# The last unit of a long convolution in pieces of 256, 128 and 128 channels in place of two halves

## The chip, the cores and the metric

The kernel runs on one core of one Trainium2 chip. The metric is the device time of one execution in microseconds (us), lower is better; the median of several executions is compared. The engines are called as in the profile: PE multiplies matrices (TensorE; PEld is its loading of stationary operands), DVE is VectorE, ACT is ScalarE, POOL is GpSimd, and SP (SyncE) only issues transfers here.

## The reference, cut to what matters

Two transformer-like blocks over 1024 positions of width 1024. The first has a mixer and a mixture of experts; the second has a linear recurrence, two gated long convolutions, a merge of the two branches, and again a mixture of experts. The change lies in the long convolutions of the second block:

```python
def fftconv(u, k, bias):
    L = u.shape[1]
    U = jnp.fft.rfft(u, n=2 * L, axis=1)
    K = jnp.fft.rfft(k, axis=0)
    y = jnp.fft.irfft(U * K[None], n=2 * L, axis=1)[:, :L]
    return y + u * bias.astype(jnp.float32)
...
        z = v.astype(f32)
        for n, gate in enumerate((x1, x2)):
            k = bidir_kernel(filt[:, n, 0], filt[:, n, 1])
            z = gate.astype(f32) * fftconv(z, k, filt_bias[l, n])
        y_b = z.astype(dt) @ w_b_out[l]
```

`y_b` is then gated and added to the other branch, multiplied by `w_o`, added to `x`, normed, routed, and sent through 16 experts.

## The kernel before, in words

The whole program is one launch, stage after stage. Each stage gives every engine its own list of instructions; the engines meet only through semaphores, and each engine goes through its list in order. DVE operations that need the one before them are chained: `c.then` has the operation raise a semaphore, and the next waits for it.

A long convolution is done by a Fourier transform written as matrix products. The channels go in halves of HC = 512, and with two orders of convolution this makes NP = 4 passes (n = 0 to 3; pass n is order n // 2, half n % 2). The length is split in RADIX = 4 residues and the frequencies in HF = 2 halves `fh`. One "unit" is one pair (n, fh): PE makes the spectrum of the input, ACT copies it to SBUF, and DVE runs `unit_butterflies` (and for a filter made in place also `filter_butterflies`): it combines the residues, multiplies by the filter's spectrum K, and combines again. The result H lies in the place of the input spectrum U. For the last unit, n = 3 and fh = 1, that place is the tile `hytab_filt`. A unit's last DVE operation, line 4304, raises `h_ready`.

Then PE transforms back in `results(n)`, in BANKS = 8 banks per pass: bank = 2 * i + half. For the second order of convolution (n = 2, 3) bank 2i and 2i + 1 take the channels `bass.ts(i, P)`, the i-th 128 of the 512, for half of the residues. There are two PSUM buffers `inv_ps` for all banks, so a bank waits until the one two before it has been read out: `pe.wait_ge(*evicted(...))`. In pass 2 ACT reads them out, in pass 3 DVE does: `result(n, bank)`, line 4566, multiplies by the gate.

The last unit was already cut in two before the change: `butterflies` takes `at` and `width` (a range of channels). The unit's first half, channels 0 to 255, releases banks 0 to 3; its second half releases banks 4 to 7. Within the second half `unit_butterflies` calls `between(4)` to `between(7)` after each of its four big products (lines 4284 and 4286), and there DVE does `result(3, 0)` to `result(3, 3)`.

After the last unit DVE's list goes on with the start of the merge (`merge.begin`, lines 3535, 3543 and 3539, five operations of 1024 columns that have nothing to do with pass 3), and then with the results of banks 4 to 7, each followed by what `merge.after` gives:

```python
    def begin(m, dve):
        m.gate_z(dve, 0)
        m.gate_z(dve, 1)
        m.rest_of_first_w(dve)
        m.rest_of_z(dve, 0)
        m.gate_z(dve, 2)
```

When the eighth bank is done, PE begins the merge's product (line 2751). SP waits for all banks and for all results of DVE (`sp.wait_ge(z_ready, N_READY)`) before it issues the merge's transfers. POOL and ACT have nothing between PE and DVE in pass 3.

Of the kernel before, what the change touches and what calls it, by code (L numbers as in the profile page):

```python
# [3673 lines left out]
RADIX = 4  # L3674
HQ = T // RADIX
HJ = HQ // P
HF = HQ // P
HC = BANK
# [650 lines left out]
def hyena_phase(nc, block, m, tab, inputs, merge, v_x1, x2_T, z1):  # L4329


    NP = len(PASSES)
# [8 lines left out]
    def k_made(n, fh):  # L4341
        return place["K", n, fh] + RADIX
# [4 lines left out]
    BANKS = 2 * RADIX  # L4347
# [19 lines left out]
    fwd_copied, product_ready, h_ready = tab.fwd_copied, tab.product_ready, tab.h_ready  # L4367
# [9 lines left out]
    @block.sync  # L4377
    def _(sp):
        def load_u(n, fh):
            o, h = PASSES[n]  # L4380
            for i in SLOTS:
                v = RADIX * (HF * n + fh) + i
                before = v - N_CHUNKS

                sp.wait_ge(fwd_made, place["U", before // RADIX // HF, before // RADIX % HF] + before % RADIX + 1)
                if o and fh == 0:

                    made = RADIX * (n - 2) + i
                    sp.wait_ge(z_stored[made % 2], 16 * (made // 2 + 1))
                sp.dma_start(u[v % N_CHUNKS][:, :, :], residues(z1 if o else v_x1, RESIDUE[i], h)).then_inc(u_loaded[v % N_CHUNKS], 16)  # L4390

        for what, n, fh in program:
            if what == "U" and (n, fh) != (0, 0):
                load_u(n, fh)
                if n == 0:

                    sp.wait_ge(inputs.proj_made, inputs.n_proj)
                    tab.load_k(sp, K, 0, fh)
                elif n not in MADE:

                    sp.wait_ge(product_ready, HF * (n - 1) + fh + 1)
                    tab.load_k(sp, K, n, fh)
                if (n, fh) == (1, 0):
                    tab.load_inverse(sp)
                if (n, fh) == (2, 0):

                    for b in range(2):
                        sp.wait_ge(tab.filt_stored[b], 16 * (NT // 2))
                    sp.wait_ge(fwd_made, k_made(MADE[0], HF - 1))
                    sp.dma_start(filt[:, :, :, :, :], tab.filters).then_inc(filt_loaded, 16)  # L4410
# [37 lines left out]
    @block.tensor  # L4448
    def _(pe):
        def spectrum(q, fh, terms, src):  # L4450

            if q >= 2:

                pe.wait_ge(fwd_copied, q - 1)
            for c in (RE, IM):
                sums = [(kind, src(part, r, j), j) for kind, part, r in terms[c] for j in range(HJ)]
                for s, (kind, rhs, j) in enumerate(sums):
                    last = nc.tensor.matmul(fwd_ps[q % 2][:, c, :], tr[:, j, kind, fh, :], rhs, start=(s == 0), stop=(s == len(sums) - 1))
            last.then_inc(fwd_made, 1)

        def filter_spectra(n, fh):

            if n == MADE[0]:
                pe.wait_ge(tab.filt_ready, len(FILTER_STEPS))
            else:
                pe.wait_ge(filt_loaded, 16)
            for i in SLOTS:
                spectrum(place["K", n, fh] + i, fh, K_TERMS[i], lambda part, r, j: filt[:, part, j, r, :])

        def input_spectra(n, fh):  # L4470
            for i in SLOTS:
                v = RADIX * (HF * n + fh) + i
                r = RESIDUE[i]
                chunk = u[v % N_CHUNKS]
                pe.wait_ge(u_loaded[v % N_CHUNKS], 16 * (v // N_CHUNKS + 1))
                spectrum(place["U", n, fh] + i, fh, ([(COS_OF[r], 0, r)], [(SIN_OF[r], 0, r)]), lambda part, r, j: chunk[:, j, :])

        def results(n):
            o, h = PASSES[n]
            H = [U_of(n, fh) for fh in range(HF)]  # L4480

            pe.wait_ge(h_ready, HF * (n + 1))
            for bank in range(BANKS):
                i, half = bank // 2, bank % 2
                e = BANKS * n + bank
                if n == NP - 1 and bank == BANKS // 2:

                    pe.wait_ge(h_ready, HF * NP + 1)
                if e >= 2:

                    pe.wait_ge(*evicted((e - 2) // BANKS, (e - 2) % BANKS))
                out = inv_ps[e % 2]
                terms = [(fh, c) for fh in range(HF) for c in (RE, IM)]
                if o == 0:
                    for fh, c in terms:
                        last = nc.tensor.matmul(out[:, :], inv[:, fh, RESIDUE[i], c, bass.ts(half, P)], H[fh][:, i, c, :],
                                                start=((fh, c) == terms[0]), stop=((fh, c) == terms[-1]))
                else:
                    for k in range(2):
                        r = 2 * half + k  # L4500
                        for fh, c in terms:
                            last = nc.tensor.matmul(out[:, bass.ts(k, HQ)], H[fh][:, RESIDUE[r], c, bass.ts(i, P)], inv[:, fh, r, c, :],
                                                    start=((fh, c) == terms[0]), stop=((fh, c) == terms[-1]))
                last.then_inc(inv_made, 1)

        pe.wait_ge(tab.tr_loaded, 16 * HJ)
        pe.wait_ge(inputs.rows_ready, inputs.n_rows)
        pe.wait_ge(tab.filt_ready, len(FILTER_STEPS))
        for what, n, fh in program:
            if what == "K":  # L4510
                filter_spectra(n, fh)
            elif what == "U":
                if (n, fh) != (0, 0):
                    input_spectra(n, fh)
            else:
                if n == 0:
                    pe.wait_ge(tab.inv_loaded, 16)
                    pe.wait_ge(inputs.raw_ready, inputs.n_raw)
                results(n)
# [29 lines left out]
    @block.vector  # L4549
    def _(dve):  # L4550
        c = inputs.unit

        def result(n, bank):

            o = PASSES[n][0]
            i, half = bank // 2, bank % 2
            e, chunk = BANKS * n + bank, RADIX * n + i
            if o == 0:
                dve.wait_ge(gate_loaded[chunk % 2], 16 * (chunk // 2 + 1))
                part, made = z[chunk % 2][:, bass.ts(half, HC)], inv_ps[e % 2][:, :]  # L4560
            else:
                dve.wait_ge(x2_loaded[i], 16)
                part = merge.z.whole[:, RADIX + i, :].rearrange("p (q r) -> p r q", r=RADIX)[:, bass.ts(half, 2), :]
                made = inv_ps[e % 2][:, :].rearrange("p (r q) -> p r q", r=2)
            dve.wait_ge(inv_made, e + 1)
            dve.tensor_tensor(part, made, part, ALU.mult).then_inc(z_ready, 1)

        def butterflies(n, fh, back, first_bank=0, at=0, width=HC):

            g = HF * n + fh
            k, x = (w[:, :, :, bass.ds(at, width)] for w in (K[fh][:, :, :, :], U_of(n, fh)))
            by = cross[:, :, :, bass.ds(at, width)]

            def back_to(bank):
                if back is not None and bank >= first_bank:
                    result(back, bank - first_bank)

            def filter_made(dve):  # L4580
                dve.wait_ge(fwd_copied, k_made(n, fh))
                filter_butterflies(c, k)

            def filter_loaded(dve):
                dve.wait_ge(tab.k_loaded[fh], 16 * (n // HF + 1))

            k_ready = filter_made if n in MADE else filter_loaded
            if n in MADE and place["K", n, fh] < place["U", n, fh]:
                k_ready(dve)
                k_ready = lambda dve: None  # L4590
            dve.wait_ge(fwd_copied, u_made(n, fh))
            unit_butterflies(c, tab, g, k, x, by, width, k_ready, back_to, at != 0)

        dve.wait_ge(inputs.conv_ready, inputs.n_conv)
        for n in range(1, NP):
            butterflies(n - 1, 1, 0 if n - 1 == 1 else None)
            butterflies(n, 0, n - 1 if n - 1 == 1 else None)
        butterflies(NP - 1, 1, None, width=HC // 2)
        butterflies(NP - 1, 1, NP - 1, first_bank=4, at=HC // 2, width=HC // 2)
        merge.begin(dve)  # L4600
        for bank in range(BANKS // 2, BANKS):
            result(NP - 1, bank)
            merge.after(dve, bank)
# [302 lines left out]
```

## Time and profile before

| what | value |
|---|---|
| median of 3 runs | 3942.96 us (3939.01 to 3943.96) |
| the profiled execution | 3944.96 us, its span 3943.2 us |
| mean granted clock of PE | 0.973 |
| PE busy | 3710.8 us, 94% of the span |
| DVE busy | 2842.8 us, 72% |
| ACT busy | 1857.6 us, 47% |

The span is the time from the first to the last instruction that the profiler recorded; the profiled execution's own time is 1.76 us above it. The table is over the whole program, and the stage of the change is some 75 us of it, from about 2500 to 2575 us. There the trace is read in order of time: a row of the timeline has its start, its length, engine, line, operation, output <- inputs, shapes and count; a bracket at its end tells how long its engine was idle before it and what ended that. Like instructions that follow each other are merged in one row, xN being their number. In the profile one fp32 matmul is two records.

### The profile page before, as it was taken

What the parts mean: (1) busy time and instruction counts of PE and PEld (TensorE: products, weight loads), DVE (VectorE), ACT (ScalarE), POOL (GpSimd) and SP (SyncE); (2) the same over time, 40 slices, a digit from 0 to 9 for tenths busy, and PEclk for the clock granted to TensorE, in tenths of its full rate; (3) what the DMA queues carried; (4) which work ended last, traced back from release to release, by engine and by line L of the source; (5) the groups of instructions that cost most, each with busy time, mean ns of one, the idle gap of its engine ahead of it and who ended that gap; (6) DMA issues with size and microseconds to landing.
All of it is one profiled execution on the core that took longest, in us unless ns stands there. A gap on an engine that the chain in (4) does not pass through costs nothing. (4 is left out here: it accounts for less than half of the span.)

```text
span 3943.2 us, 42184 instructions
## 1 busy us (share of the span) xinstructions
PE 3710.8 (94%) x16780; PEld 2853.3 (72%) x16780; DVE 2842.8 (72%) x2581; ACT 1857.6 (47%) x1719; POOL 264.3 (7%) x281
## 2 busy tenths in 40 slices
PE   8989998799999799999999989899499999999998
PEld 3557776688888677777887634587288888888886
DVE  2655445889888675655345899954799898889887
ACT  3243431687777334443011111210377777777776
POOL 0000000100000200000000000000000101010100
PEclk9999999899999899999999999899799999999999
DMA  3003024899998632223344515143599999999998
GB/s 119 6 14 114 22 77 170 322 419 415 417 414 348 235 124 69 67 67 102 97 122 142 200 58 192 54 160 129 215 371 385 384 389 382 387 381 389 385 385 311
DMA packets 367168, 891.04 MB, mean 226 GB/s; under 512 B 21994, under 2 KB 118609, under 8 KB 357556
## 3 DMA queue, kind: packets, MB, share of 16 engines
q1 hardware_dynamic: 323796, 758.12, 51.7%
q0 software_dynamic: 26896, 97.17, 7.0%
q10 hardware_dynamic: 16336, 33.82, 2.2%
q8 instruction: 97, 1.59, 0.2%
q14 instruction: 43, 0.35, 0.0%
HBM read 788.65 MB, written 100.40 MB: 225 GB/s over the span
## 5 line engine op out<-in xcount | busy, mean ns | idle before, releaser
L2342 DVE TENSOR_TENSOR moe_w_rest<-moe_w_w,moe_upper 128x2048 fp32r<-128x2048 f32 x384 | 862.4, 2288 | 132.3 <-ACT moe_upper L2251 66.4
L2243 ACT ACTIVATE moe_upper<-moe_w_w 128x2048 fp32r<-128x2048 f32 x192 | 357.4, 1909 | 229.2 <-PE moe_y_ps L2207 103.2
L2342 DVE TENSOR_TENSOR moe_w_rest<-moe_w_w,moe_upper_w 128x2048 fp32r<-128x2048 f32 x192 | 430.6, 2284 | 14.0 <-ACT moe_upper_w L2261 13.9
L2261 ACT ACTIVATE moe_upper_w<-moe_w_w 128x2048 fp32r<-128x2048 f32 x192 | 357.5, 1910 | 116.5 <-PE moe_up_ps L2181 74.7
L2251 ACT ACTIVATE moe_upper<-moe_w_w 128x2048 fp32r<-128x2048 f32 x192 | 356.7, 1911 | 3.0 <-DMA moe_w_w<-in_w_up_dram 2.8
L2181 PE MATMUL moe_up_ps<-moe_upper,moe_x_upper 128*128 128x512 f32 x768 | 308.4, 402 | 0.0
L2181 PE MATMUL moe_gate_ps<-moe_upper,moe_x_upper 128*128 128x512 f32 x768 | 300.5, 391 | 4.7 <-DVE moe_x_rest L2355 4.7
L2181 PE MATMUL moe_gate_ps<-moe_upper,moe_x_rest 128*128 128x512 f32 x768 | 300.1, 391 | 0.0
L2181 PE MATMUL moe_up_ps<-moe_upper,moe_x_rest 128*128 128x512 f32 x768 | 299.9, 391 | 0.0
L2181 PE MATMUL moe_gate_ps<-moe_w_rest,moe_x_upper 128*128 128x512 f32 x768 | 299.9, 390 | 0.0
L2181 PE MATMUL moe_up_ps<-moe_w_rest,moe_x_upper 128*128 128x512 f32 x768 | 298.9, 389 | 0.0
L2207 PE MATMUL moe_y_ps<-moe_upper_w,moe_hidT_upper 128*128 128x512 f32 x760 | 295.9, 389 | 1.9 <-DVE moe_hidT_rest L2360 1.9
L2207 PE MATMUL moe_y_ps<-moe_upper_w,moe_hidT_rest 128*128 128x512 f32 x760 | 295.7, 389 | 0.0
L2207 PE MATMUL moe_y_ps<-moe_w_rest,moe_hidT_upper 128*128 128x512 f32 x760 | 295.7, 389 | 0.0
L2181 PEld LDWEIGHTS moe_gate_ps<-moe_upper,moe_x_upper 128*128 128x128 f32 x768 | 144.9, 189 | 35.6 <-DVE moe_x_rest L2355 5.5
L2181 PEld LDWEIGHTS moe_up_ps<-moe_upper,moe_x_rest 128*128 128x128 f32 x768 | 144.1, 188 | 31.7
L2181 PEld LDWEIGHTS moe_gate_ps<-moe_w_rest,moe_x_upper 128*128 128x128 f32 x768 | 145.0, 189 | 30.1
L2181 PEld LDWEIGHTS moe_gate_ps<-moe_upper,moe_x_rest 128*128 128x128 f32 x768 | 144.8, 189 | 30.3
L2207 PEld LDWEIGHTS moe_y_ps<-moe_upper_w,moe_hidT_upper 128*128 128x128 f32 x760 | 142.7, 188 | 32.1 <-DVE moe_hidT_rest L2360 2.7
L2181 PEld LDWEIGHTS moe_up_ps<-moe_w_rest,moe_x_upper 128*128 128x128 f32 x768 | 144.6, 188 | 27.3
L2207 PEld LDWEIGHTS moe_y_ps<-moe_upper_w,moe_hidT_rest 128*128 128x128 f32 x760 | 142.7, 188 | 29.7
L2207 PEld LDWEIGHTS moe_y_ps<-moe_w_rest,moe_hidT_upper 128*128 128x128 f32 x760 | 142.7, 188 | 29.5
(636 smaller groups left out, 7524.7 us busy)
## 6 DMA issues: line engine op xcount, KB each, us to landing
moe_w_w<-in_expert_w_dram SPq DMA_DIRECT2D x96, 2048.0 KB, 10.6
moe_w_w<-in_w_gate_dram SPq DMA_DIRECT2D x64, 2048.0 KB, 11.5
moe_w_w<-in_w_up_dram SPq DMA_DIRECT2D x64, 2048.0 KB, 10.8
moe_w_w<-in_w_down_dram SPq DMA_DIRECT2D x64, 2048.0 KB, 10.8
tmp_y_rows<-moe_y ACTq DMA_DIRECT2D x32, 512.0 KB, 9.0
block_w_first<-in_w_in_dram SPq DMA_DIRECT2D x20, 512.0 KB, 3.8
tmp_h<-out_xn POOLq DMA_DIRECT2D x16, 512.0 KB, 2.9
tmp_spectra<-held_K ACTq DMA_DIRECT2D x8, 1024.0 KB, 4.7
```

What stands on the lines that cost most here:

```text
L2181: last = nc.tensor.matmul(out[:, :], lhs[:, k, :], rhs[:, k, :], start=(k == 0 and n == 0), stop=(k == ND - 1 and n == 2))
L2207: last = nc.tensor.matmul(m.y_ps[:, h, :], lhs[:, k, :], rhs[:, k, bass.ts(h, BANK)], start=(start and k == 0 and n == 0), stop=(stop and ...
L2243: act.activation(half(upper1(c), h), half(weights.w1[c % 2], h), ACT.Copy).then_inc(m.w1_rounded, 1)
L2251: act.activation(half(upper3(c), h), half(weights.w3[c % 2], h), ACT.Copy).then_inc(m.w3_rounded, 1)
L2261: act.activation(half(upper2(i, c), h), half(weights.w2[c % 2], h), ACT.Copy).then_inc(m.w2_rounded, 1)
L2342: dve.tensor_tensor(half(rest, h), half(whole, h), half(upper, h).bitcast(F32), ALU.subtract).then_inc(done, 1)
```

## The change

Where the last unit was done in two pieces (256 and 256 channels), it is now done in three (256, 128 and 128). The four results that lay within the second piece lie within the second still. PE now waits for `h_ready` at bank 4 (second piece) and again at bank 6 (third piece).

```diff
@@ in results(n), the list of PE
-                if n == NP - 1 and bank == BANKS // 2:
+                if n == NP - 1 and bank >= BANKS // 2 and half == 0:
 
-                    pe.wait_ge(h_ready, HF * NP + 1)
+                    pe.wait_ge(h_ready, HF * NP + 1 + bank // 2 - RADIX // 2)
                 if e >= 2:
 
                     pe.wait_ge(*evicted((e - 2) // BANKS, (e - 2) % BANKS))
@@ the list of DVE
         butterflies(NP - 1, 1, None, width=HC // 2)
-        butterflies(NP - 1, 1, NP - 1, first_bank=4, at=HC // 2, width=HC // 2)
+        butterflies(NP - 1, 1, NP - 1, first_bank=4, at=HC // 2, width=HC // 4)
+        butterflies(NP - 1, 1, None, at=3 * HC // 4, width=HC // 4)
         merge.begin(dve)
         for bank in range(BANKS // 2, BANKS):
             result(NP - 1, bank)
             merge.after(dve, bank)
```

What stands on DVE where the second piece ends, before the change (`hytab_filt` is H of the last unit, `merge_z` and `merge_x` are the merge's gated inputs, `hyena_inv_ps` is a bank):

```order
L3813 TENSOR_TENSOR hytab_filt<-hytab_filt 128x256
L4260 TENSOR_TENSOR hytab_filt<-hytab_filt 128x256
L3818 SCALAR_TENSOR_TENSOR hytab_filt<-hytab_filt 128x256
L4304 SCALAR_TENSOR_TENSOR hytab_filt<-hytab_filt 128x256
L3535 TENSOR_TENSOR merge_z<-merge_z,merge_x_0 128x1024
L3535 TENSOR_TENSOR merge_z<-merge_z,merge_x_1 128x1024
L3543 TENSOR_TENSOR merge_w_rest<-merge_w,merge_w_upper 128x1024
L3539 TENSOR_TENSOR merge_z_rest<-merge_z,merge_z_upper 128x1024
L3535 TENSOR_TENSOR merge_z<-merge_z,merge_x_2 128x1024
L4566 TENSOR_TENSOR merge_z<-hyena_inv_ps,merge_z 128x2x256
```

And what stands there now, from the second piece's last four operations on (`hyena_K` is the filter's spectrum):

```order
L3813 TENSOR_TENSOR hytab_filt<-hytab_filt 128x128
L4260 TENSOR_TENSOR hytab_filt<-hytab_filt 128x128
L3818 SCALAR_TENSOR_TENSOR hytab_filt<-hytab_filt 128x128
L4304 SCALAR_TENSOR_TENSOR hytab_filt<-hytab_filt 128x128
L3813 TENSOR_TENSOR hyena_K<-hyena_K 128x2x128
L3818 SCALAR_TENSOR_TENSOR hyena_K<-hyena_K 128x2x128
L3813 TENSOR_TENSOR hyena_K<-hyena_K 128x4x128
L3818 SCALAR_TENSOR_TENSOR hyena_K<-hyena_K 128x2x128
L3818 SCALAR_TENSOR_TENSOR hyena_K<-hyena_K 128x128 x2
L3813 TENSOR_TENSOR hytab_filt<-hytab_filt 128x2x2x128
```

The second piece's operations have half the columns, and behind its last one (line 4304) come the 33 operations of the third piece, six on K and 27 on H; only then the rows from line 3535 on follow as before. So the merge's five operations and the result of bank 4 have moved behind 33 more operations.

On PE the two lists differ in one wait. This is the beginning of bank 6 (the names of semaphores are those of earlier stages, whose semaphores are used again: `norm1_xn_ready` is the evicted bank, `att_in_n_split` is `h_ready`):

```order
 L4502 MATMUL hyena_inv_ps<-hytab_inv,hyena_U 128x256 x2
 L4502 MATMUL hyena_inv_ps<-hytab_inv,hytab_filt 128x256 x2
-L4502 MATMUL hyena_inv_ps<-hytab_inv,hyena_U 128x256 [waits norm1_xn_ready]
+L4502 MATMUL hyena_inv_ps<-hytab_inv,hyena_U 128x256 [waits norm1_xn_ready,att_in_n_split]
 L4502 MATMUL hyena_inv_ps<-hytab_inv,hyena_U 128x256
 L4502 MATMUL hyena_inv_ps<-hytab_inv,hytab_filt 128x256 x2
```

No matmul has moved; bank 6 has the wait for the third piece beside the wait for the read-out of bank 4, which it had before.

## Rows read from the trace of the kernel before

**Rows 1.** The page's first line: the span.
```profile
span 3943.2 us, 42184 instructions
```
**Rows 2.** Timeline of DVE: the last unit and the merge's beginning.
```profile
2500.34 0.68 DVE L3813 TENSOR_TENSOR hyena_K<-hyena_K 128x512 f32<-128x512 f32 x1
...
2524.73 0.68 DVE L3813 TENSOR_TENSOR hyena_K<-hyena_K 128x512 f32<-128x512 f32 x1
...
2535.08 1.23 DVE L4284 TENSOR_TENSOR hyena_cross<-hytab_filt,hyena_K 128x1024 f32<-128x1024 f32 x1
2536.34 1.06 DVE L4566 TENSOR_TENSOR merge_z<-hyena_inv_ps,merge_z 128x512 f32<-128x512 f32 x1
2537.31 1.22 DVE L4286 TENSOR_TENSOR hytab_filt<-hytab_filt,hyena_K 128x1024 f32<-128x1024 f32 x1
...
2542.90 1.09 DVE L4566 TENSOR_TENSOR merge_z<-hyena_inv_ps,merge_z 128x512 f32<-128x512 f32 x1 [0.69 <-PE hyena_inv_ps L4502]
...
2546.35 1.06 DVE L4566 TENSOR_TENSOR merge_z<-hyena_inv_ps,merge_z 128x512 f32<-128x512 f32 x1 [1.23 <-PE hyena_inv_ps L4502]
...
2548.76 0.69 DVE L3813 TENSOR_TENSOR hytab_filt<-hytab_filt 128x512 f32<-128x512 f32 x1
...
2554.84 2.35 DVE L3535 TENSOR_TENSOR merge_z<-merge_z,merge_x 128x1024 f32<-128x1024 f32 x2
...
2559.38 1.22 DVE L3535 TENSOR_TENSOR merge_z<-merge_z,merge_x 128x1024 f32<-128x1024 f32 x1
2561.86 1.08 DVE L4566 TENSOR_TENSOR merge_z<-hyena_inv_ps,merge_z 128x512 f32<-128x512 f32 x1 [1.26 <-PE hyena_inv_ps L4502]
```
**Rows 3.** Timeline of PE: the eight banks of pass 3, then the merge's product.
```profile
2524.86 2.08 PE L4502 MATMUL hyena_inv_ps<-hytab_inv,hyena_U 128*128 128x256 f32 x4 [5.48 <-DVE hytab_filt L4304]
...
2531.17 1.03 PE L4502 MATMUL hyena_inv_ps<-hytab_inv,hyena_U 128*128 128x256 f32 x4
...
2537.46 2.08 PE L4502 MATMUL hyena_inv_ps<-hytab_inv,hyena_U 128*128 128x256 f32 x4 [2.67 <-DVE merge_z L4566]
...
2554.98 2.08 PE L4502 MATMUL hyena_inv_ps<-hytab_inv,hyena_U 128*128 128x256 f32 x4 [8.76 <-DVE hytab_filt L4304]
...
2561.59 1.03 PE L4502 MATMUL hyena_inv_ps<-hytab_inv,hyena_U 128*128 128x256 f32 x4
...
2571.08 1.03 PE L4502 MATMUL hyena_inv_ps<-hytab_inv,hytab_filt 128*128 128x256 f32 x4
2571.76 0.58 PE L2751 MATMUL merge_b_ps<-merge_z_upper,merge_w_upper 128*128 128x512 f32 x1
```
**Rows 4.** DVE's groups by form: count, then busy us, mean ns, idle before.
```profile
L3818 DVE SCALAR_TENSOR_TENSOR hytab_filt<-hytab_filt 128x512 f32<-128x512 f32 x12 | 8.3, 693 | 0.4
...
L3818 DVE SCALAR_TENSOR_TENSOR hytab_filt<-hytab_filt 128x256 f32<-128x256 f32 x6 | 2.6, 425 | 0.2
...
L977 DVE SCALAR_TENSOR_TENSOR gla_o_n<-gla_banks,gla_rstd,gla_gate 128x128 f32<-128x128 f32 x32 | 9.0, 345 | 0.7
...
L1372 DVE CUSTOM_DVE_ANT_0 att_logit<-att_score,att_bias 128x128 f32<-128x128 f32 x8 | 2.3, 286 | 4.5 <-ACT att_prob L1312 4.5
```
**Rows 5.** Windows at the starts of banks 0, 2 and 4; PEclk is the granted clock.
```profile
2524.86:2530.36 5.50, 5.50 (x13) 4.43 (x14) 5.26 (x8) 0.00 (x0) 0.00 (x0) 0.50 0.32 129
...
2537.46:2540.20 2.74, 2.74 (x7) 2.20 (x8) 2.71 (x3) 0.00 (x0) 0.00 (x0) 0.50 0.00 0
...
2554.98:2561.00 6.02, 6.02 (x14) 4.86 (x15) 5.62 (x5) 2.48 (x3) 0.00 (x0) 0.50 0.00 0
```
**Rows 6.** Timelines behind the last bank: SP's first transfer, DVE's and PE's waits.
```profile
2573.34 0.35 SPq L3591 DMA_DIRECT2D merge_gate<-tmp_gate_T  x1
...
2594.53 0.69 DVE L130 CAST merge_w_upper<-merge_w 128x1024 fp32r<-128x1024 f32 x1 [7.79 <-DMA merge_w<-in_w_b_out_dram]
...
2596.61 0.49 PE L2751 MATMUL merge_b_ps<-merge_z_upper,merge_w_upper 128*128 128x512 f32 x1 [2.73 <-DVE merge_w_rest L133]
```
**Rows 7.** A window in the last mixture of experts: PE, PEld, DVE, ACT, POOL busy.
```profile
3000.00:3050.00 50.00, 50.00 (x232) 41.56 (x231) 43.49 (x25) 36.98 (x25) 1.19 (x2) 1.00 1.04 395
```

## The prediction, made before the changed kernel was run

> **What bounds the kernel now.** The whole-program table does not answer this; the stage does. I read the timelines of PE and DVE side by side, then the windows for PE's clock, then what follows the last bank. In the last unit DVE works nearly without a gap from 2500.34 us on [rows 2], and PE stands before it: 5.48 us before bank 0, 2.67 us before bank 2 and 8.76 us before bank 4, each time until DVE is done with something [rows 3]. From bank 4 on it turns round: PE runs banks 4 to 7 and goes straight into the merge's product at 2571.76 [rows 3], while DVE waits for PE before its results (1.26 us at 2561.86) [rows 2]. So the chain through this stage is: first piece on DVE, second piece on DVE, then four banks on PE. It ends when bank 7 ends, at 2571.08 + 0.86 = 2571.94, where 0.86 is the distance of two such rows (four of them make one bank, below).
>
> What comes behind takes any shift along. SP issues the merge's transfers only at 2573.34, after the last result; a later one of these loads is what DVE waits 7.79 us for at 2594.53, and PE then waits 2.73 us for DVE [rows 6]. These transfers are issued in answer to the last result and to PE's products, so they move with bank 7 and cannot hide a delay. The final mixture of experts has PE busy for all 50 us of a 50 us window [rows 7]; no slack there gives time back. I therefore take the shift of bank 7's end as the shift of the program's end.
>
> **The change, part by part.** All that stands before 2524.73 is as before, the first piece included (it took 2524.73 - 2500.34 = 24.39 us) [rows 2].
>
> Price of a piece. A piece has 33 operations. Counting their columns for 256 channels: 6 operations of 1024, 17 of 512 and 10 of 256, in all 17408. The 512-column form takes 693 ns and the 256-column form 425 ns [rows 4], so 256 columns are worth 268 ns, 1.04 ns each, or 18.1 us for 17408. The remaining 24.39 - 18.1 = 6.3 us are fixed, 0.19 us for each of 33 operations. A piece of 128 channels has the same 33 operations with half the columns: 6.3 + 9.05 = 15.3 us. Two of them cost 30.6 us in place of 24.4: the change adds 6.3 us to DVE.
> No chained 128-column operation is in the trace. By the line through the two forms it takes 425 - 134 = 291 ns; the nearest rows are 286 ns (SBUF output, 128 columns) and 345 ns (PSUM input) [rows 4]. I take 291; at 345 each of the 14 such operations that count below costs 54 ns more, 0.8 us in all, at 286 0.1 us less.
>
> Second piece, now 128 channels wide. PE's banks 0 to 3 need only the first piece. Bank 0 starts at 2524.86 and takes 6.31 us at half clock, bank 1 starts at 2531.17 [rows 3]. A bank at full clock takes (2571.94 - 2561.59) / 3 = 3.45 us [rows 3]. Before, DVE came to the first result only at 2536.34, (2535.08 - 2524.73) = 10.35 us of operations and one of 1024 columns after the piece's start [rows 2]. Now those first 15 operations have half the columns (7168 fewer to 3584, which saves 3.7 us) and the sixteenth 512 fewer (0.5 us); the first result starts at about 2532.1. That is before PE has finished bank 1 (2531.17 + 3.45 = 2534.62), so PE does not wait before bank 2 and keeps its clock: bank 3 ends at 2531.17 + 3 x 3.45 = 2541.5. With the same lag of a result behind its bank, DVE starts the fourth result at 2541.8 in place of 2546.35 [rows 2]. Here 4.5 us are won, in a place where PE now sets the pace, so that the rest of the second piece's saving (9.1 us of columns in all) is lost in DVE's waits.
> Behind the fourth result: 0.97 us for it (2537.31 - 2536.34 [rows 2]); two operations of 256 columns at 0.46 with the step between operations, 0.92; and the tail of ten operations. The tail took 2554.84 - 2548.76 = 6.08 us [rows 2] with 4096 columns; with 2048 it takes 2.13 less, 3.95. The second piece ends at 2541.8 + 0.97 + 0.92 + 3.95 = 2547.65. PE can start bank 4 there, 7.2 us earlier than before. This is all that the change gains, and it is not yet at the end of the chain.
>
> Third piece: no results lie in it, DVE waits for nobody: 2547.65 + 15.3 = 2562.95. PE meanwhile does banks 4 and 5 (6.6 + 3.45 us, until about 2557.8) and then stands, because both PSUM buffers are full.
>
> The merge's five operations come next on DVE, before it empties bank 4. They take 2559.38 + 1.22 - 2554.84 = 5.76 us [rows 2]. Before, they lay under bank 4's own 6.61 us on PE (2561.59 - 2554.98 [rows 3]) and cost nothing; DVE even waited 1.26 us behind them [rows 2]. That cover is gone: bank 4 has long been made, and bank 6 waits for its read-out. DVE starts that result at 2562.95 + 5.76 = 2568.7, it lasts 1.08 [rows 2], and PE starts bank 6 0.06 us later (2537.46 against 2536.34 + 1.06 [rows 2, 3]), at 2569.85. The new wait for the third piece, over at 2563, costs nothing beside it.
>
> Banks 6 and 7. PE has then stood about 12 us. After 5.48 and 8.76 us of standing the granted clock was 0.50 for the first 5.50 and 6.02 us [rows 3, 5], 1.2 of 2.4 GHz, so bank 6 costs what bank 4 did, 6.61, and bank 7 3.45: the end is 2569.85 + 10.06 = 2579.9. Bank 7 waits for the result of bank 5, which DVE does 3.4 us behind that of bank 4, long under bank 6. Against 2571.94 bank 7 ends 8.0 us later. From the other side: bank 6 starts 14.9 us later than bank 4 did, and two full-clock banks (6.9) fewer stand behind it.
>
> The sum: the profiled execution's span of 3943.2 us [rows 1], time 3944.96, becomes 3952.9. It lies 2.0 us above the median of 3942.96, so for the median I give 3942.96 + 8.0 = 3951.0.
>
> **A price weighed against the skill.** Rows 4 put the fixed part of a DVE operation at 425 - 267 = 158 ns, 0.19 us with the step to the next. The Trainium skill (VectorE: DVE Perf Modes, section on the TRN2 errata) has a table by which an SBUF operation costs 58 cycles beside its columns at 0.96 GHz, some 60 ns, and says below it that measured fixed parts are about 150 cycles and that tiles should have 512 elements or more. By its table the change would cost about 4 us; by this trace the table's figure is wrong for these operations (256 columns took 425 ns, not 327), and its advice speaks against the change.
>
> **The rivals.**
> 1. *Shorter stretch at half clock.* At bank 2 the clock was 0.50 for 2.74 us only [rows 5], not 5.5 to 6. If bank 6 gets so short a stretch, it saves half the difference, (6.02 - 2.74) / 2 = 1.6 us: 3949.4, 6.4 us slower. If bank 0 gets it too, bank 3 ends 1.4 us earlier and DVE's chain with it: 3948.0. Against it: both long stands of rows 3 had the long stretch, and bank 6 follows the longest. The Trainium skill (TensorE: Matmul & The Clock Gate, part 1) says that the number of cold matmuls at a start varies from run to run of one kernel; rows 5 show three stretches of two lengths within one run.
> 2. *Dear small operations.* At the 345 ns of rows 4 and with bank 4's start late by as much: 0.8 us more, 3951.8; a further microsecond if the step between short chained operations is not the 0.03 us that it is at 256 columns: 3953.
> 3. *Not slower: bank 6 does not wait for the read-out.* If PE could start bank 6 as soon as the third piece is done, at 2562.95 + 0.05, bank 7 would end at 2573.1, 1.1 us later than before: 3944.1; with full clock it would even be 2 us earlier. It decides the sign from the point at which bank 4 is emptied before DVE reaches 2560. Against it stands DVE's list: the result of bank 4 is behind the third piece and the merge's five operations.
> 4. *The delay is taken up behind.* The transfers that DVE waits 7.79 us for [rows 6] would have to be issued by something that does not move. Half of the delay gone would be 3947. Nothing in rows 6 speaks for it.
> 5. *Cheap operations.* If 128-column operations had a fixed part of 60 ns in place of 158, the third piece and the tail would be 43 x 0.1 = 4.2 us shorter: 3946.8. Rows 4 speak against it at 128 columns too (286 and 345 ns).
>
> **How the numbers follow.** Chances: the forecast with rival 2, 0.68, at 3951 (its own range 3949.5 to 3953); rival 1 0.18; rival 3 0.03; rival 4 0.06; rival 5 0.03; something else 0.02. A measurement of this kernel tells about 0.2% from no change, 7.9 us, and that is just the size forecast. Medians of three scatter by 1 to 2 us (the runs lie between 3939.01 and 3943.96). So within the forecast the chance to be above 7.9 us is a little over 0.6 with the dear side counted, some 0.45 of the whole; rival 1 adds 0.04: slower 0.49. Faster by 0.2% would need 7.9 us that only rival 3 points to and by far does not reach: 0.02. The rest, 0.49, is within 0.2%. The range is 3945.5 to 3954.5: at its low end it takes in rivals 1, 4 and 5 with the scatter, at its high end rival 2.
>
> **What would show it.** On the timeline of the changed kernel: DVE's pieces of 128 channels of 15.3 us without results, with 128-column operations near 291 ns; no wait of PE before bank 2, and DVE waiting for PE before the results of banks 1, 2 and 3; bank 4 starting near 2547.7; PE idle about 12 us before bank 6, put down to DVE's result at line 4566 and not to line 4304; bank 6 at half clock; the merge's product starting near 2579.8. The prediction is wrong if bank 6 starts before 2565, or if the loads behind the last result land as early as before.

## The result and the profile after

The changed kernel is slower by about what was forecast: median 3948.55 us (3946.24 to 3958.4, 9 runs) against 3942.17 us (3939.01 to 3946.97, 9 runs), ratio 1.002 with a 95% interval of 1.0011 to 1.0029. Run again (below) it came to 3952.0 us against 3944.13, ratio 1.0022 (1.0013 to 1.0032). So 6.4 and 7.9 us were measured where 8.0 were forecast; both intervals leave out 1.

The profiled execution alone would mislead: its span is 3943.5 us, 0.3 us above [rows 1], and with 3946.24 us it is the fastest of its nine runs. The stage says more. DVE's timeline in the changed kernel:

```profile
2495.11 0.69 DVE L3813 TENSOR_TENSOR hyena_K<-hyena_K 128x512 f32<-128x512 f32 x1
...
2519.49 0.42 DVE L3813 TENSOR_TENSOR hyena_K<-hyena_K 128x256 f32<-128x256 f32 x1
...
2526.84 1.08 DVE L4566 TENSOR_TENSOR merge_z<-hyena_inv_ps,merge_z 128x512 f32<-128x512 f32 x1
...
2531.93 1.09 DVE L4566 TENSOR_TENSOR merge_z<-hyena_inv_ps,merge_z 128x512 f32<-128x512 f32 x1 [0.81 <-PE hyena_inv_ps L4502]
...
2535.38 1.05 DVE L4566 TENSOR_TENSOR merge_z<-hyena_inv_ps,merge_z 128x512 f32<-128x512 f32 x1 [1.76 <-PE hyena_inv_ps L4502]
...
2541.21 0.42 DVE L3813 TENSOR_TENSOR hyena_K<-hyena_K 128x256 f32<-128x256 f32 x1
...
2556.51 2.35 DVE L3535 TENSOR_TENSOR merge_z<-merge_z,merge_x 128x1024 f32<-128x1024 f32 x2
...
2561.06 1.21 DVE L3535 TENSOR_TENSOR merge_z<-merge_z,merge_x 128x1024 f32<-128x1024 f32 x1
2562.19 1.08 DVE L4566 TENSOR_TENSOR merge_z<-hyena_inv_ps,merge_z 128x512 f32<-128x512 f32 x1
```

The last unit begins 5.2 us earlier than in [rows 2], in a program whose list up to there is the same: that much the stages ahead differ from one execution to the next (in the ten profiles of this document it begins between 2495.11 and 2502.64 us), and here it hides the loss. Counted from each trace's own first row, the third piece begins at 46.1 us and takes 2556.51 - 2541.21 = 15.30 us, the merge's five operations 5.68 us, and the result of bank 4 starts at 67.1 us.

PE's timeline of the changed kernel:

```profile
2519.62 2.07 PE L4502 MATMUL hyena_inv_ps<-hytab_inv,hyena_U 128*128 128x256 f32 x4 [6.65 <-DVE hytab_filt L4304]
...
2524.72 1.03 PE L4502 MATMUL hyena_inv_ps<-hytab_inv,hyena_U 128*128 128x256 f32 x4
...
2541.34 2.07 PE L4502 MATMUL hyena_inv_ps<-hytab_inv,hyena_U 128*128 128x256 f32 x4 [6.10 <-DVE hytab_filt L4304]
...
2550.11 1.03 PE L4502 MATMUL hyena_inv_ps<-hytab_inv,hytab_filt 128*128 128x256 f32 x4
2563.41 2.04 PE L4502 MATMUL hyena_inv_ps<-hytab_inv,hyena_U 128*128 128x256 f32 x4 [12.28 <-DVE merge_z L4566]
...
2568.79 1.03 PE L4502 MATMUL hyena_inv_ps<-hytab_inv,hyena_U 128*128 128x256 f32 x4
...
2571.38 1.03 PE L4502 MATMUL hyena_inv_ps<-hytab_inv,hytab_filt 128*128 128x256 f32 x4
2572.05 0.58 PE L2751 MATMUL merge_b_ps<-merge_z_upper,merge_w_upper 128*128 128x512 f32 x1
```

No wait stands before bank 2 any more. Bank 4 starts early, bank 5 ends, and then PE stands 12.28 us, released by DVE's result (line 4566) and not by the third piece (line 4304). The merge's product starts 76.94 us after the unit's first row, against 71.42 from [rows 2, 3]: 5.5 us later.

The windows of the changed kernel at the starts of banks 0 and 6 and in the merge's third tile, columns as in [rows 5]:

```profile
2519.62:2522.90 3.28, 3.28 (x8) 2.65 (x9) 3.08 (x7) 0.00 (x0) 0.00 (x0) 0.52 0.24 97
2563.41:2567.00 3.59, 3.58 (x9) 2.85 (x10) 3.59 (x4) 1.44 (x2) 0.00 (x0) 0.50 0.00 0
2599.00:2601.50 2.50, 2.50 (x8) 1.91 (x7) 2.46 (x4) 0.00 (x0) 0.00 (x0) 0.54 0.36 106
```

The half clock of banks 0 and 6 lasted 3.3 and 3.6 us, where [rows 5] have 5.50 and 6.02 at banks 0 and 4.

### The profile page after: what moved, and what is told of

It reads as the page before. It is cut to its first block and busy times, and to the rows that moved or that the text cites. A ratio compares the mean times of both kernels' runs of the same rounds, so it can differ in the third digit from the quotient of the medians.

```text
span 3943.5 us, 42219 instructions
## 1 busy us (share of the span) xinstructions
PE 3705.2 (94%) x16780; PEld 2850.0 (72%) x16780; DVE 2847.2 (72%) x2614; ACT 1858.0 (47%) x1719; POOL 264.3 (7%) x281
## 5 line engine op out<-in xcount | busy, mean ns | idle before, releaser
L2342 DVE TENSOR_TENSOR moe_w_rest<-moe_w_w,moe_upper 128x2048 fp32r<-128x2048 f32 x384 | 862.3, 2288 | 132.4 <-ACT moe_upper L2251 69.5
## 6 DMA issues: line engine op xcount, KB each, us to landing
moe_w_w<-in_w_up_dram SPq DMA_DIRECT2D x64, 2048.0 KB, 10.6
moe_w_w<-in_w_down_dram SPq DMA_DIRECT2D x64, 2048.0 KB, 10.6
```

What stands on the lines that cost most here:

```text
L2342: dve.tensor_tensor(half(rest, h), half(whole, h), half(upper, h).bitcast(F32), ALU.subtract).then_inc(done, 1)
```

## The experiments

All were timed beside the kernel before on the same chip. "Stage" is the time from DVE's first operation of the last unit to the first matmul of the merge's product, "SP" the time from the same start to SP's first transfer of the merge, "to the end" the time from the same start to the end of the span. These three are read from one profiled execution of each kernel, and those of the changed kernel and of its repetition differ by 1.9 us in the stage. Totals are differences of medians, and the ratios are computed from the runs in another way, so the two can differ by some 2 us.

| kernel | stage us | SP us | to the end, us | total against before, us | ratio (95%) |
|---|---|---|---|---|---|
| before | 71.42 | 73.00 | 1442.9 | | |
| changed | 76.94 | 78.57 | 1448.4 | +6.4 | 1.0020 (1.0011 to 1.0029) |
| changed, again | 78.86 | 80.45 | 1453.4 | +7.9 | 1.0022 (1.0013 to 1.0032) |
| one release | 78.71 | 80.34 | 1450.9 | +7.4 | 1.0021 (1.0012 to 1.0030) |
| banks 4 and 5 read first | 72.20 | 75.62 | 1445.1 | +4.0 | 1.0013 (1.0004 to 1.0022) |
| 384 + 128, banks 4 and 5 read first | 63.55 | 69.94 | 1440.8 | -2.0 | 0.9999 (0.9990 to 1.0008) |
| 384 + 128, old order | 72.07 | 73.70 | 1446.7 | +1.2 | 1.0002 (0.9993 to 1.0011) |
| 384 + 128, all results first | 63.77 | 65.60 | 1435.2 | -7.2 | 0.9982 (0.9973 to 0.9991) |
| changed, PE kept busy | 75.00 | 76.62 | 1446.8 | +5.0 | 1.0007 (0.9998 to 1.0016) |
| 384 + 128, all first, PE kept busy | 63.06 | 64.90 | 1434.7 | -8.0 | 0.9978 (0.9969 to 0.9987) |

**The changed kernel again.** Nothing is changed in it.

> The changed kernel once more, as it is, beside the kernel before on the same chip; it says how well 0.1% can be told. The stage is measured on the timelines from DVE's first operation of the last unit to the first matmul of the merge's product; before it is 71.4 us. My theory (two more costs on DVE, the merge's five operations uncovered, two banks left on PE behind them): 77 to 79 us, so 5.5 to 8 us more than before, the spread coming from how long PE runs at half clock after its stands. Rival (the program's total is moved by something outside the stage): the stage again near 77, but the total not 5 to 8 us above that of before.

The stage took 78.86 us, 7.4 more than before, and the total was 7.9 us above. It differs from the first profile where the theory says: at the two half-clock starts. The windows of this run at banks 0 and 6:

```profile
2526.89:2532.40 5.51, 5.51 (x13) 4.43 (x14) 5.10 (x13) 0.00 (x0) 0.00 (x0) 0.50 0.12 48
2571.96:2577.00 5.04, 5.04 (x12) 4.05 (x13) 4.25 (x4) 2.89 (x4) 0.00 (x0) 0.50 0.00 0
```

5.5 and 5.0 us at half clock here, 3.3 and 3.6 there, after stands of much the same length (6.62 and 13.34 us against 6.65 and 12.28). A row of four records in PE's timeline lasts 2.07 us at half clock and 1.03 at full clock (rows above), so each microsecond at half clock costs half a microsecond; the two differences together make (2.2 + 1.4) / 2 = 1.8 of the 1.9 us between the two stages.

**One release.** The three pieces stay, PE waits for both later ones at bank 4:

```diff
-                if n == NP - 1 and bank >= BANKS // 2 and half == 0:
+                if n == NP - 1 and bank == BANKS // 2:
 
-                    pe.wait_ge(h_ready, HF * NP + 1 + bank // 2 - RADIX // 2)
+                    pe.wait_ge(h_ready, HF * NP + 2)
```

> The three pieces stay, but PE waits at bank 4 for the second and the third piece together, so that the early release of bank 4 is taken away. Theory (the early release is worth nothing, since bank 6 waits for DVE to empty bank 4 behind the third piece and the merge's five operations): bank 4 starts where the third piece ends, 61.3 us into the stage, four banks of 3.45 us and 1.7 to 3.2 us of half clock follow: 76.8 to 78.3 us, the same as the changed kernel, total 5.5 to 8 us above before. Rival (two banks made ahead are two banks saved): 6.9 us longer than the changed kernel, 84 us, total 12 to 15 us above before.

78.71 us, the same as the changed kernel's 78.86 in the same comparison, and the total is 0.5 us from it, inside its interval. PE stood before bank 4 for as long as it could and lost nothing by it:

```profile
2564.32 2.08 PE L4502 MATMUL hyena_inv_ps<-hytab_inv,hyena_U 128*128 128x256 f32 x4 [21.39 <-DVE hytab_filt L4304]
```

So the early release, which is what the change buys, is worth nothing in this order. Two banks made ahead (6.9 us of PE) are paid back by the 5.7 us of merge operations and the read-out of bank 4, which now stand between the third piece and bank 6. That these two come out equal, at 6.9 us each, is chance; by the same sum the early release would gain something if less work stood there. No run has one release together with the read-outs first, so that gain is not shown by itself.

**Banks 4 and 5 read first.** One move on DVE, in the changed kernel:

```diff
+        result(NP - 1, BANKS // 2)
+        result(NP - 1, BANKS // 2 + 1)
         merge.begin(dve)
         for bank in range(BANKS // 2, BANKS):
-            result(NP - 1, bank)
+            if bank >= BANKS // 2 + 2:
+                result(NP - 1, bank)
             merge.after(dve, bank)
```

> The changed kernel with one move on DVE: the results of banks 4 and 5 stand in front of the merge's first five operations, right behind the third piece. Theory (the five operations lost their cover and hold back bank 6): bank 6 starts 1.1 us behind the third piece in place of 6.9 us, so the stage takes 71.4 to 72.7 us and the total is 0 to 1.5 us above before, 5 to 6 us below the changed kernel. Rival (what costs is the third piece's fixed 6.3 us on DVE alone, and the order of the merge's operations does nothing since they have to be done anyway): 76 to 77 us, 5 to 6 us above before.

The stage is 72.20 us, in the range of the theory, and not 76 to 77. PE's wait before bank 6 has halved (it was 12.28 and 13.34 us):

```profile
2560.42 2.05 PE L4502 MATMUL hyena_inv_ps<-hytab_inv,hyena_U 128*128 128x256 f32 x4 [6.64 <-DVE merge_z L4566]
```

The total went down by only 3.8 us against the changed kernel, 1 to 2 less than expected, and stands 4.0 us above before where 0 to 1.5 were expected: SP's first transfer stands at 75.62 us, 2.6 behind before where the product is 0.8 behind, since DVE's last result now follows more work. That was an oversight of mine: I had taken bank 7 and the last result as one thing.

**384 and 128 channels, banks 4 and 5 read first.** The order on DVE is that of the experiment above; the pieces are:

```diff
-        butterflies(NP - 1, 1, None, width=HC // 2)
-        butterflies(NP - 1, 1, NP - 1, first_bank=4, at=HC // 2, width=HC // 4)
-        butterflies(NP - 1, 1, None, at=3 * HC // 4, width=HC // 4)
+        butterflies(NP - 1, 1, None, width=3 * HC // 4)
+        butterflies(NP - 1, 1, NP - 1, first_bank=4, at=3 * HC // 4, width=HC // 4)
```

and PE's one wait for the second piece stands at bank 6.

> Two pieces again, of 384 and 128 channels: banks 0 to 5 wait for the first, banks 6 and 7 for the second; the four results lie within the second piece as before, and the results of banks 4 and 5 stand in front of the merge's five operations. By the prices per piece (33 operations at 0.19 us, 1.04 ns a column): first piece 33.5 us; the second waits for PE's banks 0 to 3 and ends at 56.2 us of the stage; PE has then just made bank 5, bank 6 starts at 57.3 us at full clock and bank 7 ends at 64.2 us. Theory: stage 63.5 to 65.5 us, total 6 to 8 us below before. Rival (the end of the stage is set by DVE's total work, which is that of before): stage 70 to 72 us, total as before.

The stage came out as worked out, 63.55 us, 7.9 below before. The total did not: it is 2.0 us below before where 6 to 8 were expected, and the interval of its ratio takes in 1, that is, no difference. The gain is lost behind the stage, in the merge (timelines of DVE and PE of this run):

```profile
2593.26 0.69 DVE L130 CAST merge_w_upper<-merge_w 128x1024 fp32r<-128x1024 f32 x1 [8.36 <-DMA merge_w<-in_w_b_out_dram]
...
2595.35 0.79 PE L2751 MATMUL merge_b_ps<-merge_z_upper,merge_w_upper 128*128 128x512 f32 x1 [3.43 <-DVE merge_w_rest L133]
```

The windows of the same run over that tile:

```profile
2594.00:2596.50 2.50, 1.15 (x3) 0.96 (x4) 2.47 (x3) 0.00 (x0) 0.00 (x0) 0.50 0.63 185
2596.50:2599.00 2.50, 2.50 (x8) 1.93 (x7) 2.50 (x3) 0.00 (x0) 0.00 (x0) 0.50 0.16 22
```

SP's first transfer is only 3.1 us earlier than before, and the third tile of the merge starts at 93.4 us of the count against 96.3 ([rows 6] less the first of [rows 2]): 2.9 us are left of 7.9. Then PE, which stood 3.43 us for the weights, runs the beginning of that tile at half clock; DVE's line 3656 follows 13.96 us behind the one before it, against 11.44 in the kernel before. Another 2.5 us are gone, and 0.4 are left there (107.15 against 107.50 us of the count). The end of the span is 2.1 us earlier; where the later stages won the rest was not followed.

**384 and 128 channels, old order.** The same cut, with the merge's five operations in front of the results as in the kernel before. Against that kernel:

```diff
-                if n == NP - 1 and bank == BANKS // 2:
+                if n == NP - 1 and bank == BANKS // 2 + 2:
...
-        butterflies(NP - 1, 1, None, width=HC // 2)
-        butterflies(NP - 1, 1, NP - 1, first_bank=4, at=HC // 2, width=HC // 2)
+        butterflies(NP - 1, 1, None, width=3 * HC // 4)
+        butterflies(NP - 1, 1, NP - 1, first_bank=4, at=3 * HC // 4, width=HC // 4)
```

> Two pieces of 384 and 128 channels, but with the merge's five operations in front of the results of banks 4 and 5, as in the kernel before and the changed one. It tells how much of the gain of the 384 and 128 version was the cut and how much the order. Theory (bank 6 waits for DVE to empty bank 4, and the five operations stand before that): the second piece ends 55.5 us into the stage, bank 6 starts at 62.4 and not at 56.8, on a clock that has fallen: the merge's product starts at 71.0 to 72.3 us, as before the change (71.4), and the total is within 1.5 us of before. Rival (the cut alone does it): 63.5 to 65 us.

72.07 us, and 1.2 us in the total: no better than before. The cut alone gives nothing; the 8.5 us between this and the version above come from the order of the read-outs. Of these 5.7 are the wait itself (bank 6 starts at 62.46 us of the stage against 56.76), and 2.8 are the half clock that follows it (from there to the product it takes 9.61 us against 6.79). PE stood 6.00 us before bank 6:

```profile
2558.50 2.04 PE L4502 MATMUL hyena_inv_ps<-hytab_inv,hyena_U 128*128 128x256 f32 x4 [6.00 <-DVE merge_z L4566]
```

**384 and 128 channels, all results first.** Against the version with banks 4 and 5 read first:

```diff
         merge.begin(dve)
-        for bank in range(BANKS // 2, BANKS):
-            if bank >= BANKS // 2 + 2:
-                result(NP - 1, bank)
+        for bank in range(BANKS // 2 + 2, BANKS):
+            result(NP - 1, bank)
+        for bank in range(BANKS // 2, BANKS):
             merge.after(dve, bank)
```

> The 384 and 128 version with the results of banks 6 and 7 too in front of what followed banks 4 and 5 on DVE (four operations of 1024 columns). There the merge's product had started 7.9 us earlier than before the change, but SP's transfers only 3.1 us earlier, since SP waits for DVE's last result. Theory (behind the stage the time hangs on these transfers and on the clock, so the gain must reach SP): the product starts near 63.6 us of the stage again, SP's first transfer at 65 to 66 us in place of 69.9, total 4 to 7 us below before. Rival (PE now waits in the merge's product for the operations that were moved back, and nothing is won): total 0 to 2 us below before, as measured for that version.

The product starts at 63.77 us as before this edit, SP's transfer at 65.60 in place of 69.94, and the total is 7.2 us below before, ratio 0.9982 (0.9973 to 0.9991): faster than both kernels, though by less than 0.2% of the whole. PE waits 1.20 and 0.61 us in the product for the operations that were moved back, as the rival had it, but that is all of it. The third tile begins at 89.00 us of the count, 7.3 before the 96.27 of the kernel before, so nearly the whole 7.7 us of the stage have come through, and PE stands only 0.68 us before it:

```profile
2567.05 0.50 PE L2751 MATMUL merge_b_ps<-merge_z_upper,merge_w_upper 128*128 128x512 f32 x1 [1.20 <-DVE merge_z_rest L3539]
...
2569.32 0.50 PE L2751 MATMUL merge_b_ps<-merge_z_upper,merge_w_upper 128*128 128x512 f32 x1 [0.61 <-DVE merge_z_rest L3539]
...
2589.34 0.49 PE L2751 MATMUL merge_b_ps<-merge_z_upper,merge_w_upper 128*128 128x512 f32 x1 [0.68 <-DVE merge_w_rest L133]
```

**The changed kernel with PE kept busy.** Unused matmuls of the same shape as the real ones, before bank 0 (12) and before bank 6 (27), with a wait until ACT has emptied the buffer that they write:

```diff
+            def keep_busy(times):
+                for _ in range(times):
+                    nc.tensor.matmul(fwd_ps[0][:, 0, 0:HQ], inv[:, 0, 0, 0, 0:P], inv[:, 0, 0, 1, :], start=True, stop=True)
+
+            if n == NP - 1:
+                pe.wait_ge(fwd_copied, N_ALL_FWD)
+                keep_busy(12)
...
+                if n == NP - 1 and bank == BANKS // 2 + 2:
+                    keep_busy(27)
                 if n == NP - 1 and bank >= BANKS // 2 and half == 0:
```

> The changed kernel, with work on PE that nobody uses: 12 fp32 matmuls of 256 columns before bank 0 of pass 3 and 27 before bank 6, into a PSUM buffer that is free by then, so that PE does not stand there. Theory (what my prediction had too large was the time at half clock behind the two stands, and it is also what makes the stage differ between runs): banks 0 and 6 run at full clock from their start, 3.45 us each; the stage is 73 to 74.5 us against 77 to 79 for the changed kernel, the total 3.5 to 5.5 us below it. Rival (the granted clock does not depend on what PE did before, or the added matmuls delay the real ones by as much): 77 us or more.

Bank 6 began at full clock; this window is its start and bank 7:

```profile
2570.84:2577.60 6.76, 6.76 (x31) 5.97 (x32) 6.49 (x6) 3.90 (x4) 0.00 (x0) 1.00 0.01 2
```

The stage is 75.00 us, 1.9 and 3.9 below the two profiles of the changed kernel. That is half a microsecond above my range. By the medians the total is 1.4 to 2.9 us below that of the changed kernel and not 3.5 to 5.5, by the ratios (1.0007 against 1.0020 and 1.0022) it is 5 to 6 us below; the ratios' intervals overlap, so the total does not settle the matter where the stage does. My range was wrong at bank 0: keeping the clock there gains little, since PE then waits 1.15 us for DVE's first read-out before bank 2. DVE's fourth result starts at 40.15 us, against 40.27 in the first profile of the changed kernel and 41.54 in the repeated one: 0.1 and 1.4 us. The larger part of the gain is behind the start of bank 6, from where the product is reached in 6.80 us against 8.64 and 9.27: 1.8 and 2.5 us.

**384 and 128 channels, all results first, PE kept busy** with 30 such matmuls before bank 0, and none before bank 6:

```diff
+            if n == NP - 1:
+                pe.wait_ge(fwd_copied, N_ALL_FWD)
+                keep_busy(30)
```

> The version with 384 and 128 channels and all results first, with 30 unused matmuls on PE before bank 0, where PE stands 14 us. By rows of that version bank 0 loses 1.5 to 3 us to half clock, and DVE waits 2.9 us in the second piece for banks 1 to 3. Theory: these waits shrink by about the time that bank 0 gains; DVE's second piece ends up to 1.5 to 2 us earlier, and the stage is 61.5 to 63 us. Rival (bank 3 is bound by DVE's read-out of bank 1 and not by bank 0): no change, 63.6 us.

63.06 us, 0.7 less than without them, a little short of the theory's range (61.5 to 63) and more than by its rival (no change); two profiles of one kernel differed by more, and the total of -8.0 us is not to be told from -7.2. What ties the 0.7 us to the clock is that DVE's fourth result starts at 49.19 in place of 49.91 us. DVE's wait before the fourth result stayed at 1.77 us: banks 2 and 3 follow DVE's read-outs, and only the shorter waits ahead of them shrank.

## Why the prediction was right

1. *DVE's second and third piece* (15.3 us for the third): right. It took 15.30 us. The 128-column operations take what the line through the two longer forms gave, 291 ns, as the groups of the changed kernel show:

```profile
L3818 DVE SCALAR_TENSOR_TENSOR hytab_filt<-hytab_filt 128x128 f32<-128x128 f32 x6 | 1.8, 292 | 0.2
L3813 DVE TENSOR_TENSOR hytab_filt<-hytab_filt 128x128 f32<-128x128 f32 x4 | 1.2, 293 | 0.1
```

 The rival of dear small operations and that of cheap ones (60 ns fixed) are both out: 292 ns less 128 columns at 1.04 is 159 ns. The table of the Trainium skill (VectorE: DVE Perf Modes, section on the TRN2 errata) is off here by 98 ns in each; its sentence on about 150 cycles, an estimate of 156 ns at 0.96 GHz, fits.

2. *4.5 us won in the second piece, bank 4 earlier by 7.2 us*: right in kind. Bank 4 started at 46.2 and 47.5 us of the stage in the two profiles, against 54.6 before and 47.4 forecast, and DVE's fourth result at 40.3 and 41.5, against 46.0 before and 41.5 forecast. PE did not wait before bank 2. DVE waited for PE before the results of banks 1, 2 and 3, as forecast, in the repeated profile; in the first one, where bank 0 was shorter, before those of banks 2 and 3 alone.

3. *This gain does not reach the end, since bank 6 waits for DVE to empty bank 4 behind the merge's five operations*: right, and shown from two sides. Taking the early release away changed nothing (78.71 against 78.86 us); taking the five operations away from between gave back 6.7 us of the stage (78.86 to 72.20), of which 0.9 us is the clock (DVE's fourth result starts at 40.2 us in the one and 41.5 in the other, bank 6 takes 6.4 and 6.0) and 5.7 the order (from the start of the third piece's last operation to bank 6 it is 1.40 us in the one and 7.12 in the other), where 5.8 had been worked out (6.9 - 1.1). Bank 6 started 68.3 and 69.6 us after the unit's first row, where the forecast had 69.5. By the bare time of the trace, 2563.41 us, the first profile lies below the 2565 that the prediction named as a sign against itself; that sign had not allowed for a unit that begins 5.2 us earlier, and counted from the unit's start and set on the time of the kernel before it is 2500.34 + 68.30 = 2568.6.

4. *Banks 6 and 7 cost 10.06 us, bank 6 at half clock for as long as bank 4 was before*: bank 6 did start at half clock after the stand, but this term was mis-sized, by 1.2 us in the first profile (2563.41 to 2572.24, the last row's start with 0.86, is 8.83 us) and 0.6 in the repeated one (9.45). Bank 0 was also 1.2 us shorter in the first profile (5.10 against 6.31), and this is the whole of 5.5 against 8.0 us: 8.0 - 1.2 - 1.2 = 5.6. In the repeated one 8.0 - 0.6 = 7.4 us came out. It is the first rival in part: its 6.4 us for a short stretch at bank 6 are just what the first comparison of medians gave, and the repeated one, 7.9, is nearly the forecast's 8.0.

5. *What comes behind takes the shift along*: right for a shift of all of PE, DVE and SP together: in the two profiles the span from the unit's first row on is 5.5 and 10.6 us longer, where the stage is 5.5 and 7.4. It is not exact. In the first one, PE stood 2.86 us in the merge and a part of its third tile ran at half clock (0.54 on average over the last window above), where the kernel before stood 2.73 us [rows 6] and its clock was not lowered:

```profile
2599.00:2601.50 2.50, 2.50 (x12) 2.06 (x11) 2.47 (x3) 0.00 (x0) 0.00 (x0) 1.00 0.51 169
```

 This added 1.6 us to that execution (line 3656 comes 13.05 us behind the one before it, against 11.44), and the same to the repeated one (13.02, after a stand of 3.08 us). I had no such term. So it is partly luck that the totals came so near to 8.0 us: the half clock in the stage had been put too high, by 0.6 to 2.4 us, and this 1.6 us had been put at nothing. What then remains, 1.6 us less in the first and 1.6 us more in the second, lies in later stages and was not followed.

## What to carry to other kernels

Cutting work finer so that a consumer can begin earlier pays only up to the next thing the consumer needs. Here that was an empty buffer, and it stood in the producer's list behind work that had been free as long as the consumer was busy. Before a unit is cut, list what stands between the early release and the next buffer, and move the read-outs ahead of it; with that, fewer and unequal pieces (384 and 128) gave 7.2 us where three pieces had cost 6.4 to 7.9. Look also at what a transfer queue waits for: a stage that PE leaves 7.9 us earlier is worth 2 us if the last read-out, on which the next loads hang, does not come earlier too.

## What the runs showed of the hardware that had not been expected

PE's half clock after a stand is not of one length: after stands of 6.65, 6.62 and 5.48 us bank 0 had 3.3, 5.5 and 5.5 us at 1.2 GHz. Nor does it grow with the stand: behind the 21.39 us of the version with one release it was 4.8 us.

Whether the clock falls at all does not follow from the length of the stand either. In the merge, 2.73 us (kernel before) and 2.78 us (384 and 128 channels, old order) left it at full speed and 2.86 us did not; before bank 2 of the kernel before it was lost with a stand of 2.67 us [rows 3, 5]. A stand of only 1.87 us lost it, in the version of the changed kernel with banks 4 and 5 read first, while 2.02 us in the version with 384 and 128 channels and banks 4 and 5 read first did not. This is the start of the merge's second tile in the former, and a window behind it:

```profile
2583.24 0.69 PE L2751 MATMUL merge_b_ps<-merge_z_upper,merge_w_upper 128*128 128x512 f32 x1 [1.87 <-DVE merge_w_rest L133]
```

```profile
2583.40:2586.50 3.10, 3.10 (x8) 2.42 (x9) 2.47 (x3) 1.19 (x2) 0.00 (x0) 0.50 1.02 408
```

In the changed kernel's third tile the clock fell only after PE had begun again: 0.8 us at full speed came first, in the window from 2597.06 to 2597.86 us. What decides between these cases the runs do not show.
